# An encoder block on one core: the next expert's transposes moved by a column, a tile load moved ahead of a wait, affinities kept in SBUF, and Newton steps on GpSimd at the end

## The reference, cut to what matters

```python
mixed = (jax.nn.sigmoid(g_a) * jnp.matmul(o_g, w_o_gqa)
         + jax.nn.sigmoid(g_b) * jnp.matmul(o_m, w_o_mla))
h = h + jnp.matmul(mixed, w_out)
...
t = _rmsnorm(h, ffn_norm).reshape(n, D)
aff = jax.nn.softmax(jnp.matmul(t, w_router).astype(jnp.float32), axis=-1)
g, idx = lax.top_k(aff.T, cap)                 # 16 experts, cap = 130 rows of each group
xs = t[idx]
hg = jnp.einsum('ecd,edf->ecf', xs, w_gate)
hu = jnp.einsum('ecd,edf->ecf', xs, w_up)
y = jnp.einsum('ecf,efd->ecd', jax.nn.silu(hg) * hu, w_down) * g[..., None]
out = jnp.zeros((n, D), y.dtype).at[idx.reshape(-1)].add(y.reshape(-1, D))
h = h + out
h = _rmsnorm(h, final_norm)                    # meta rows are dropped
```

## Time and profile before

| what | value |
|---|---|
| time, median of 3 runs | 2949.36 us (2943.27 to 2949.93) |
| the profiled execution's own time | 2949.2 us |
| its span, first to last instruction | 2947.4 us |
| busy: PE, PEld, DVE, ACT, Pool | 95%, 89%, 61%, 49%, 25% of the span |
| mean granted clock of TensorE | 0.972 |

### The profile page before, as it was taken

One profiled execution on the slowest core, in us unless ns is written; L12 is line 12 of the kernel. 1 busy time (PEld: TensorE's weight loads), 2 busy tenths in 40 slices (PEclk: granted clock), 3 DMA queues, 4 the chain that ended last, 5 costly groups with the idle time before them and its releaser, 6 DMA issues. The chain is left out here.

```text
span 2947.4 us, 54402 instructions
## 1 busy us (share of the span) xinstructions
PE 2790.1 (95%) x19748; PEld 2613.7 (89%) x19748; DVE 1811.8 (61%) x2888; ACT 1448.8 (49%) x2623; POOL 740.9 (25%) x1279
## 2 busy tenths in 40 slices
PE   8999899999999999999999999999946999999994
PEld 7888698999989999999999999988836999999994
DVE  6777766888887777775343334423354565555555
ACT  4333336888887777776222223311122445444543
POOL 0000013444442554546000000000031333323331
PEclk9999898999999999999999999999977999999997
DMA  6556493112204334553865754556645898888977
GB/s 210 154 157 191 143 385 111 49 47 73 52 23 101 90 100 127 138 148 104 239 183 162 212 161 136 143 180 195 198 126 138 203 211 200 201 198 215 204 160 266
DMA packets 534413, 466.64 MB, mean 158 GB/s; under 512 B 61907, under 2 KB 467107, under 8 KB 534257
## 3 DMA queue, kind: packets, MB, share of 16 engines
q1 hardware_dynamic: 510768, 403.68, 47.9%
q0 software_dynamic: 21120, 60.81, 9.1%
q10 hardware_dynamic: 2368, 0.16, 0.0%
HBM read 320.29 MB, written 144.21 MB: 158 GB/s over the span
## 5 line engine op out<-in xcount | busy, mean ns | idle before, releaser
L2835 PE MATMUL e_gu<-e_x_hi,w_hi 128*128 128x260 f32 x1024 | 294.2, 287 | 0.9 <-DVE e_x_lo L3040 0.9
L2835 PE MATMUL e_gu<-e_x_lo,w_hi 128*128 128x260 f32 x1024 | 290.3, 284 | 0.0
L2835 PE MATMUL e_gu<-e_x_hi,w_lo 128*128 128x260 f32 x1024 | 290.0, 283 | 0.0
L3035 DVE TENSOR_TENSOR w_lo<-w_raw,w_hi 128x2048 fp32r<-128x2048 f32 x90 | 206.3, 2292 | 100.5 <-ACT w_hi L2936 99.7
L1956 ACT ACTIVATE n_exps<-n_st_ps 128x348 f32<-128x348 f32 (+3 forms) x432 | 199.0, 461 | 120.5 <-PE n_st_ps L1901 116.0
L2039 DVE TENSOR_TENSOR n_p_lo<-n_exps,n_p_hi 128x696 fp32r<-128x696 f32 (+1 forms) x192 | 176.3, 918 | 106.4 <-ACT n_p_hi L1970 106.1
L123 POOL MEMSET s_ident<- 128x128 f32 x1 | 0.2, 209 | 779.2 <-POOLq L3247 779.2
L2835 PEld LDWEIGHTS e_gu<-e_x_hi,w_hi 128*128 128x128 f32 x1024 | 194.1, 190 | 1.1 <-DVE e_x_lo L3040 1.1
L2835 PEld LDWEIGHTS e_gu<-e_x_lo,w_hi 128*128 128x128 f32 x1024 | 194.3, 190 | 0.0
L2835 PEld LDWEIGHTS e_gu<-e_x_hi,w_lo 128*128 128x128 f32 x1024 | 193.9, 189 | 0.0
L2236 PE MATMUL c_acc<-c_tokens,c_w_back 128*128 128x260 f32 x1536 | 191.2, 284 | 2.9 <-DVE c_prod L2311 2.8
(11 more groups left out here) (344 smaller groups left out, 7751.0 us busy)
## 6 DMA issues: line engine op xcount, KB each, us to landing
c_raw<-in_w_in SPq DMA_DIRECT2D x64, 512.0 KB, 5.2
w_raw<-in_w_gate SPq DMA_DIRECT2D x64, 512.0 KB, 6.5
w_raw<-in_w_up SPq DMA_DIRECT2D x64, 512.0 KB, 8.0
w_raw<-in_w_down SPq DMA_DIRECT2D x64, 512.0 KB, 4.5
c_tokens<-hn_t SPq DMA_DIRECT2D x16, 1040.0 KB, 9.6
c_tokens<-o_t SPq DMA_DIRECT2D x32, 520.0 KB, 6.6
r_mt<-mix_t SPq DMA_DIRECT2D x32, 512.0 KB, 5.2
mix_t<-c_out_hi SPq DMA_DIRECT2D x32, 260.0 KB, 2.1
```

The source lines that it names most:

```text
L2835: ins = pe.matmul(gu[:, j % 2, a, 0:W], w[:, j, at:at + P], t[:, k, :], start=(k == 0 and q == 0), stop=(k == DK - 1 and q == 2))
L3035: dve.tensor_tensor(w_lo[:, j, :], raw[:, j % RAW, :], w_hi[:, j, :].bitcast(F32), ALU.subtract)\
```

## The change

Four edits, independent of each other:

1. In `down` the transposes of the next expert for k = 2 to 7 come after column k - 1 in place of column k - 2, on PE, ACT and DVE alike. `LATE_SLABS` stays as it is.
2. SP no longer waits for `mix`'s stores before the first loads of `residual`, but for the products; the tile of step 1 goes first, the wait for the stores follows behind the router's weights.
3. The affinities get a home in SBUF (`aff_home`, 64 x 528). From step 11 on each block is written there by DMA, and what lies in DRAM by then is copied there by four DMAs at step 11 (`load_home`); the meta columns go there last. Pool fills 16 spare columns with -1. `choose` then loads only `row_map`, and waits for it behind the rounds; the rounds work on 528 columns.
4. At the end DVE makes three of the instructions of a batch's root (`guess`), Pool the Newton steps (`refine`, 12 instructions, on Pool's program behind the last scatter), and DVE waits for Pool (`roots_ready`). Pool's gathers of the old own rows no longer wait for the last tile; they stand behind the roots of batches 0 to 2. DVE adds the own rows after tile 11, before tiles 12 to 15; the own rows' root stays on DVE.

```diff
+def refine(pool, link, v, y, a):
+    for _ in range(NEWTON):
+        link(pool.tensor_tensor(a, y, y, ALU.mult))
+        link(pool.tensor_tensor(a, a, v, ALU.mult))
+        link(pool.tensor_scalar(a, a, -0.5, 1.5, ALU.mult, ALU.add))
+        link(pool.tensor_tensor(y, a, y, ALU.mult))
...
-            sp.wait_ge(stored, 32 * DK * PASSES)
...
+            def load_home(s):
+                for g in range(GROUPS):
+                    tiles = (s - g + 1) // 2
+                    sp.wait_ge(aff_stored[g], 16 * tiles)
+                    late = (tiles - XCH // 2) * P
+                    back = (GROUPS + g) * E
+                    sp.dma_start(aff_home[g * E:(g + 1) * E, META:], scr["aff_t"][g * E:(g + 1) * E, META:FIRST_HALF])\
+                        .then_inc(gain_loaded, 16)
+                    sp.dma_start(aff_home[back:back + E, 0:late],
+                                 scr["aff_t"][g * E:(g + 1) * E, FIRST_HALF:FIRST_HALF + late]).then_inc(gain_loaded, 16)
+
+            sp.wait_ge(*mixed_done["products"])
+            load(1, 1)
             load(0, 0)
-            load(1, 1)
             sp.dma_start(gain[:, :], spread(io["ffn_norm"][0, :], 0, P)).then_inc(gain_loaded, 16)
             sp.dma_start(router[:, :, :], io["w_router"][0].rearrange("(k p) e -> p k e", p=P)).then_inc(router_loaded, 16)
+            sp.wait_ge(*mixed_done["stored"])
...
-            for part in range(2):
-                sp.dma_start(aff[part * LISTS:(part + 1) * LISTS, :], scr["aff_t"][:, part * HALF:(part + 1) * HALF])\
-                    .then_inc(loaded, 16)
...
-            dve.wait_ge(loaded, 48)
...
             link(dve.tensor_copy(column[:, :], index[:, :]))
+            dve.wait_ge(loaded, 16)
...
-                    if not is_last(e) and m + 2 < DK:
-                        tokens_of(e + 1, m + 2)
+                    if not is_last(e) and 1 <= m < DK - 1:
+                        tokens_of(e + 1, m + 1)
...
                 for m in range(DK):
                     if m % 2 == 1:
                         transposed(e, m)
-                    if m + 2 < DK:
-                        tokens(e + 1, m + 2)
+                    if 1 <= m < DK - 1:
+                        tokens(e + 1, m + 1)
                     if m in LATE_SLABS:
                         slab(e + 1, LATE_SLABS[m])
...
                 hidden(e, 2)
-                roots(0)
-                normed(0)
+                guess(0)
                 hidden(e, 3)
-                normed(1, 2)
+                roots_ready(0)
+                normed(0, 1, 2)
                 transposed(e, 1)
-                roots(1)
+                guess(1)
+                normed(3)
                 transposed(e, 3)
-                normed(3, 4)
+                roots_ready(1)
+                normed(4)
                 transposed(e, 5)
                 normed(5)
                 gates_of(e)
+                guess(2)
                 transposed(e, 7)
                 normed(6, 7)
-                roots(2)
+                roots_ready(2)
+                guess(3)
                 normed(8, 9, 10, 11)
-                roots(3)
-                normed(12, 13, 14, 15)
                 dve.wait_ge(old_gathered, 16 * NT)
...
-                roots(4)
+                roots_ready(3)
+                normed(12, 13, 14, 15)
+                own_roots()
...
+            for i in range(3):
+                roots(i)
             wait_alone(pool, x_filled, DK * E, pool_passed)
-            wait_alone(pool, row_loaded[N - 1], 16, pool_passed)
             for t in range(NT):
                 pool.indirect_dma_start(
...
+            roots(3)
```

More of the change, by code:

```diff
@@ L101, in end, with first_guess @@
         assert self.n == self.per_step, (self.n, self.per_step)
+ROOT_LINKS = 3 + 4 * NEWTON
+def first_guess(dve, link, v, mean, y):
+    link(dve.tensor_scalar(v, mean, EPS, None, ALU.add))
+    link(dve.tensor_scalar(y.bitcast(I32), v.bitcast(I32), 1, None, ALU.logical_shift_right))
+    link(dve.tensor_scalar(y.bitcast(I32), y.bitcast(I32), -1.0, float(MAGIC), ALU.mult, ALU.add))
+def refine(pool, link, v, y, a):
[4 more added lines that the diff above has]
+        link(pool.tensor_tensor(y, a, y, ALU.mult))
 def rsqrt(dve, link, v, mean, y, a):
@@ L2343, in _, with residual @@
                     body(DK - 1, 1, True)
-    return dict(products=(prod_done, NB * DK * PASSES), first_products=(prod_done, NB * DK * PASSES - 1),
+    return dict(stored=(stored, 32 * DK * PASSES), products=(prod_done, NB * DK * PASSES), first_products=(prod_done, NB * DK * PASSES - 1),
                 out_weights=(out_split_lo, DK))
-def residual(nc, io, scr, block, ident, w_out, loads, mixed_done, passed):
+AFF_AT = 226304
+def residual(nc, io, scr, aff_home, block, ident, w_out, loads, mixed_done, passed):
     N = STEPS
@@ L2399, in residual @@
         LOADS = 16 * 2
+        DIRECT = N - 6
         @block.sync
@@ L2440, in body @@
                     wait_alone(sp, at_copied, s + 1, sp_passed)
+                    if isinstance(s, int) and s == DIRECT:
+                        load_home(s)
                     if isinstance(s, int) and s == N - 1:
                         for gg in range(GROUPS):
-                            sp.dma_start(scr["aff_t"][gg * E:(gg + 1) * E, 0:META],
+                            sp.dma_start(aff_home[gg * E:(gg + 1) * E, 0:META],
                                          aff_rows[:, g, gg * META:(gg + 1) * META]).then_inc(aff_stored[g], 16)
+                    elif isinstance(s, int) and s >= DIRECT:
+                        first, at = (GROUPS + g) * E, (tile_index(s, g) - XCH // 2) * P
+                        sp.dma_start(aff_home[first:first + E, at:at + P], aff_rows[:, g, :]).then_inc(aff_stored[g], 16)
                     else:
@@ L2454, in _ @@
             sp.wait_ge(aff_stored[1], 16 * (N // 2))
+            sp.wait_ge(gain_loaded, 16 + 32 * GROUPS)
+            sp.wait_ge(router_loaded, 17)
+        @block.gpsimd
+        def _(pool):
+            pool.wait_ge(router_loaded, 16)
+            pool.memset(aff_home[GROUPS * E:, XCH // 2 * P:], -1.0).then_inc(router_loaded, 1)
         @block.tensor
@@ L2573, in _, with choose @@
             steps(dve, body, 1, 3)
-def choose(nc, io, scr, rows_t, gates_t, out_rows, w_raw, w_hi, w_lo):
+FIRST_HALF = META + TOK // 256 * P
+def choose(nc, io, scr, aff, rows_t, gates_t, out_rows, w_raw, w_hi, w_lo):
     LISTS = GROUPS * E
     ROUNDS = (CAP + 7) // 8
-    HALF = TOK // 2
     with ExitStack() as ctx:
@@ L2588, in sem @@
             return nc.alloc_semaphore("s_" + name)
-        aff = sb("aff", [2 * LISTS, HALF])
         top, index = sb("top", [2 * LISTS, ROUNDS * 8]), sb("index", [2 * LISTS, ROUNDS * 8], U32)
@@ L2748, in experts @@
             sem("gain_loaded"), [sem(f"row_loaded{n}") for n in range(N)], sem("row_squared"), sem("root_chain"), sem("marked"))
-        row_done, row_stored = sem("row_done"), sem("row_stored")
+        row_done, row_stored, own_chain = sem("row_done"), sem("row_stored"), sem("own_chain")
         old_gathered, sums_filled, sums_done, fixed, fix_stored = (
@@ L3088, in body, with own_roots @@
                         transposed(e, m)
-                    if m + 2 < DK:
-                        tokens(e + 1, m + 2)
+                    if 1 <= m < DK - 1:
+                        tokens(e + 1, m + 1)
                     if m in LATE_SLABS:
                         slab(e + 1, LATE_SLABS[m])
-            def roots(i):
-                lo, hi = BATCHES[i]
-                link = Chain(dve, root_chain, RSQRT_OPS, i)
+            def own_roots():
+                lo, hi = BATCHES[4]
+                link = Chain(dve, own_chain, RSQRT_OPS, 0)
                 dve.wait_ge(row_squared, hi)
@@ L3099, in roots, with guess, roots_ready @@
                 link.end()
+            def guess(i):
+                lo, hi = BATCHES[i]
+                at_least(dve, root_chain, ROOT_LINKS * i)
+                link = Chain(dve, root_chain, ROOT_LINKS, i)
+                dve.wait_ge(row_squared, hi)
+                first_guess(dve, link, rs[:, 0, lo:hi], mean[:, lo:hi], rs[:, 1, lo:hi])
+            def roots_ready(i):
+                dve.wait_ge(root_chain, ROOT_LINKS * (i + 1))
             def normed(*rows):
@@ L3192, in _, with roots @@
             wait_alone(pool, scattered, 16 * NT * (E - 1), pool_passed)
+            def roots(i):
+                lo, hi = BATCHES[i]
+                link = Chain(pool, root_chain, ROOT_LINKS, i)
+                link.n = 3
+                pool.wait_ge(root_chain, ROOT_LINKS * i + link.n)
+                refine(pool, link, rs[:, 0, lo:hi], rs[:, 1, lo:hi], rs[:, 2, lo:hi])
+                link.end()
+            for i in range(3):
+                roots(i)
             wait_alone(pool, x_filled, DK * E, pool_passed)
-            wait_alone(pool, row_loaded[N - 1], 16, pool_passed)
             for t in range(NT):
@@ L3239, in row_map @@
```

(7 more changed lines are left out.)

## The result

The changed kernel takes 2988.54 us (median of 4 runs, 2986.07 to 2992.6), against 2949.14 before: ratio 1.0138, 95% interval 1.0122 to 1.0154. So it is slower, as forecast, but by 39.4 us and not by 18.3, and above the stated range. The profiled execution took 2992.6 us, with a span of 2990.8, 43.4 more than that of before.

A forecast was written before the change was run, and what follows sets the result against it. The prediction took PE to bound the middle experts, busy 573.21 of 580.00 us at full clock. It summed 2949.2 + 21.7 (transposes) - 4.5 (`residual`) - 2.3 (`choose`) + 3.4 (end) to 2967.5 us, range 2955 to 2982, widened to 2952 to 2984.

The forecast's parts named there:

- The waits of the moved transposes: At the top of `gate_up`, PE waits 1.97 us for the last `x_lo`; net 1.57 a boundary, +21.7 in all.
- the gain: In `down`, the wait before the k = 2 transposes goes as their slot moves a column later: 0.4 us a boundary.
- rival (b): At the 14 expert boundaries the clock falls at each wait: 28 us more, 2995 in all; chance 0.06.
- `mix` into `residual`: Ahead of `residual`, the earlier tile load cuts PE's 3.39 us wait to 0.9 and restores the clock: -4.5 us.
- the tile of step 2: In `residual`, this tile's load stands behind step 0's work and may come late by as much as 0.7 us.
- `choose`: DVE's first `max` begins 2.8 us sooner, 51 instructions on the wider tile cost +0.5: -2.3 us.
- The end: After the last boundary, gathers behind three Pool batches lengthen the chain by 1.9, PE's wait adds 1.5: +3.4 us.
- PE's wait behind column 5: At the end, column 5's copy queues behind DVE's wait for batch 1 on Pool: up to 2.3 us, 1.5 taken.
- Pool's chain: At the end, twelve small Pool instructions a batch at 0.46 each, 5.5 us a batch.
- rival (c): At the end, DVE's scalings hold up Pool's instructions, three holds adding 3.8 us: 2971 in all; chance 0.10.
- The first gather: At the end, gathers go out after Pool ends batch 2 at 2912.4, where the first went out at 2904.95.

The follow-up runs named there:

- e5: The changed kernel with DVE alone splitting slab 4 after column 6, ACT's cast staying at column 5: 2945.9 us, ratio 1.0005.
- e3: The changed kernel with slab 4 split after column 6 in place of 5, on ACT and DVE: 2941.4 us, ratio 0.9986.
- e10: The changed kernel with slab 4's subtraction on DVE cut, three quarters ahead of the last `x_lo`, one quarter behind it: 2962.6 us, ratio 1.0052.
- e6: The kernel before with the early load of `residual`'s second tile alone: 2941.9 us, ratio 0.9981.
- e7: The kernel before with the affinities' home in SBUF and the new `choose` alone: 2943.7 us, ratio 0.9987.
- e1: The changed kernel with the token transposes back at their old columns, the other three edits kept: 2944.9 us, ratio 1.000.
- e8: The kernel before with the new end alone (Newton steps on Pool, own rows first): 2951.7 us, ratio 1.0017.
- e2: The kernel before with the moved token transposes alone: 2990.2 us, ratio 1.0156.
- e13: e12 with slab 4 split after column 4 in place of 6: 2959.9 us, ratio 1.0045.
- e9: The changed kernel with e3's slab table, all Newton steps on DVE again, gathers freed, own rows after tile 11: 2940.6 us, ratio 0.9979.
- e12: e9 with the wait for the last tile put back ahead of Pool's gathers: 2933.4 us, ratio 0.9958.

## Why the prediction was wrong

**The waits of the moved transposes: right.** 1.97 us was forecast, 1.89 measured; net of the gain 1.57 forecast and 1.8 measured (43.10 - 41.32). The path was the one described, and e5 shows that DVE's order sets it. For fourteen boundaries that is 25 us in place of 22. The term that was off is the gain: 0.4 was put for it, and 41.32 + 1.89 - 43.10 leaves 0.1. In e3, where nothing waits at `gate_up`, an expert takes 40.97, so the moved slots do give 0.35 back, and a wait costs about 0.25 more than its length: 43.10 - 40.97 = 2.13 for 1.89, and in e10, where an expert takes 42.56, 1.59 for 1.35. What the 0.25 is, no run here shows.

**The clock: the step that failed.** The sum had no term for it. It was rival (b), priced at 28 us and 2995 in all, and given 0.06. Against it stood a single row, the last boundary of the earlier trace rows, granted 1.00 after 2.04 us of idle time. That row was true and proved little: of the 14 like waits in the trace after, 11 are followed by a distance of about 44.6 to the next and 2 by 43.1, and behind the last, which has no next, the clock was granted 0.62, so equal waits go either way. At that very last boundary the traces of e6 and e7 show the clock falling behind the same 2.04, while those of e1 and e8 show it staying at 1.00. By stretch, first the kernel after behind its last long wait, then e6 behind the last boundary:

```profile
2857.60:2861.60 4.00, 3.96 (x21) 3.97 (x22) 2.49 (x3) 0.09 (x1) 3.39 (x3) 0.62 0.83 228
```

```profile
2856.00:2860.00 4.00, 3.80 (x22) 3.41 (x21) 2.96 (x5) 1.78 (x3) 0.76 (x1) 0.58 0.00 0
```

Twelve falls of 1.5 are 18 us, and the two terms together give 12 x 3.3 + 2 x 1.8 = 43 for the loop, against 42.7 by the marks. Forecast with this, the sum would have been 2949.2 + 43 - 4.5 - 2.3 + 3.4 = 2989. e10 shows how narrow the step is: behind waits of 1.35 the clock stayed at 1.00. Which of the equal waits is followed by a fall is not settled by these runs; the two without one are the sixth and the twelfth of the row after, the seventh and the thirteenth in e2.

**`mix` into `residual`: right in kind, a little small.** -4.5 forecast, -5.6 alone (e6). The wait vanished and did not just shrink to 0.9, and the tile of step 2 was not late: no wait for `mt` is left in PE's waits of the kernel after or of e6. It went whole because the tile's second half came 4.1 us sooner, counted from the last store: 2.5 by its earlier issue, and 1.6 by landing 5.7 us after its issue in place of 7.4, with both loads of `x` now behind it. The sum had the first of the two alone.

**`choose`: right.** The start moved by 2.25 us in the trace where 2.8 was forecast; -2.3 in the sum, -3.8 by e7 with an interval from -1.2 to -6.5.

**The end: the sum nearly right, its terms not.** +3.4 forecast, +4.8 in the trace, +5.0 in e8. The 1.5 put for PE's wait behind column 5 did not come: PE has no such wait in the trace after (0.5 in e8). DVE, which stood 1.61 us for batch 1, reached the copy of the gates 1.0 later than before, counted from the last boundary. Pool's chain was cheaper: instructions of 0.20 at a distance of 0.28, 3.3 us a batch and not 5.5. In return rival (c) came true: three instructions were held up by DVE's scalings, 1.23 + 1.04 + 1.12 - 3 x 0.20 = 2.8 us where 3.8 was its price. The Trainium skill, "SBUF — State Buffer", section "Who interferes with whom", has the rule that a DVE instruction with two SBUF inputs and a GpSimd instruction that reads SBUF exclude each other, so that the second to issue waits the first out. The trace agrees: the instruction at 2938.66 ends at 2939.89, just behind the scaling that ends at 2939.83. (The prediction read the 2.53 of the earlier trace rows as the writing of descriptors being held up. That issue reads its row numbers from the SBUF tile `e_rows_now` as well, so the 2.53 does not show which of the two was held.)

The first gather was issued at 2952.63, 50.2 us after the last boundary's start; forecast was 2907 + 5.5 + 1.5 = 2914, the same 50 after 2863.85. That the two agree is luck: cheap steps, holds and the missing wait cancel. From there to the first own sum it took 12.2 us (2952.63 to 2964.79) where 10.8 was put (2912.4 to 2923.2), which is the 1.4 that the end went above its forecast.

The three smaller edits sum to -4.4 by e6 to e8; together, in e1, they gave 0.0 with an interval of about 2.9 to either side. The two agree only within their intervals.

## What to carry to other kernels

Where an in-order engine splits weights between the small copies that release PE, ask for each slab what stands behind it and who waits: with the tokens at their new columns the same 2.29 us cost nothing behind column 6, 1.9 us a boundary behind column 5 and 1.4 behind column 4. A wait in a loop whose PE is otherwise full can have a second price, the clock behind it, and one boundary at full clock in a trace does not exclude it; give it a term of its own in the sum, unless several equal waits in the trace were followed by 1.00. And before a wait of a DMA for something unrelated is removed, look at which loads the DMA will then run among.

## What the runs showed of the hardware

PE's waits of 1.34 to 1.42 us left the granted clock at 1.00 at all 14 boundaries of e10 and of e13; waits of 1.86 to 1.90 did so at 2 of 14 (the kernel after, and e2 again), and at the others the expert behind took 1.5 us more. A Pool instruction of 0.20 us on a 128x4 tile took 1.04 to 1.23 beside a DVE scaling of 1.28. With four indirect gathers issued among the 16 row loads (e9), SP took 7.47 us to issue the last three of these loads; with the gathers behind them (e12), 2.84.
